# A decoder layer on one core: twelve Strassen-Winograd pairs in its MLP in place of ten, with the order of the first pieces and of the last products changed

## What is computed

```python
ff = jnp.square(jax.nn.relu(x @ w_ff1)) @ w_ff2      # w_ff1 1024 x 4096, w_ff2 4096 x 1024
x = layer_norm(2 ** 0.25 * x + ff, ln3_g, ln3_b)
```

## Time and profile before

| | before |
|---|---|
| median of 3 runs | 400.83 us (400.57 to 403.71) |
| profiled execution, device time | 401.14 us |
| its span, first to last instruction | 399.3 us |
| mean granted TensorE clock | 0.996 |
| TensorE busy | 390.9 us, 98% |
| VectorE busy | 330.2 us, 83% |
| ScalarE busy | 251.3 us, 63% |
| HBM read | 76.97 MB |

### The profile page before, as it was taken

One profiled execution on the slowest core, in us unless ns is written; L12 is line 12 of the kernel. 1 busy time (PEld: TensorE's weight loads), 2 busy tenths in 40 slices (PEclk: granted clock), 3 DMA queues, 4 the chain that ended last, 5 costly groups with the idle time before them and its releaser, 6 DMA issues.

```text
span 399.3 us, 5666 instructions
## 1 busy us (share of the span) xinstructions
PE 390.9 (98%) x2118; PEld 334.8 (84%) x2118; DVE 330.2 (83%) x430; ACT 251.3 (63%) x335; POOL 74.1 (19%) x71
## 2 busy tenths in 40 slices
PE   8999999999999999999999999999999999999993
PEld 6888888889888888899988888888888888888872
DVE  5599595999988896878567776999798979999896
ACT  6666569666464628555733776787687767776720
POOL 2059400047860105000005101000000000000000
PEclk9999999999999999999999999999999999999998
DMA  8997737734646390755353266775776575667002
GB/s 286 376 379 264 252 116 249 259 128 139 243 146 213 106 313 5 243 179 191 126 200 126 97 236 213 238 235 214 236 231 190 202 253 175 219 220 251 2 0 105
DMA packets 24449, 78.39 MB, mean 196 GB/s; under 512 B 1670, under 2 KB 3046, under 8 KB 20326
## 3 DMA queue, kind: packets, MB, share of 16 engines
q1 hardware_dynamic: 22592, 75.24, 52.5%
q0 software_dynamic: 1440, 2.62, 4.5%
q10 hardware_dynamic: 390, 0.17, 0.2%
HBM read 76.97 MB, written 1.05 MB: 195 GB/s over the span
## 4 chain that ended last, share of the span: by engine, by line
PE 81%; DMA 8%; DVE 6%; ACT 2%; issue 2%; DVEq 0%; ACTq 0%
PE bank L1560 15%; PE bank L1561 15%; PE bank L1562 15%; PE bank L1634 12%; PE bank L1963 7%; DMA raw<-in_w_ff 7%; PE bank L1638 6%; PE bank L1970 4%; DVE w_lo L1400 2%; PE bank L1786 2%; DVE w_lo L1394 1%; PE bank L1566 1%; DMA raw<-in_lead 1%; PE bank L1740 1%; DVE actB L1462 0%
## 5 line engine op out<-in xcount | busy, mean ns | idle before, releaser
L1011 DVE TENSOR_TENSOR w_lo<-raw,w_hi 128x2048 fp32r<-128x2048 f32 x30 | 70.6, 2360 | 10.9 <-ACT w_hi L609 10.8
L609 ACT CAST w_hi<-raw 128x2048 fp32r<-128x2048 f32 x32 | 60.7, 1913 | 15.9 <-PE bank L1562 14.3
L1963 PE MATMUL bank<-actA,w_hi 128*128 128x512 f32 x224 | 55.6, 391 | 0.0
L1963 PEld LDWEIGHTS bank<-actA,w_hi 128*128 128x128 f32 x224 | 41.9, 188 | 8.9 <-ACT const L918 0.3
L1560 PE MATMUL bank<-w_hi,actB 128*128 128x512 f32 x109 | 43.4, 398 | 0.0
L1561 PE MATMUL bank<-w_lo,actB 128*128 128x512 f32 x109 | 42.7, 391 | 0.0
L1562 PE MATMUL bank<-w_hi,actB 128*128 128x512 f32 x109 | 42.6, 391 | 0.0
L1560 PE MATMUL bank<-w_hi,actA 128*128 128x512 f32 x96 | 38.0, 396 | 0.0
L1562 PE MATMUL bank<-w_hi,actA 128*128 128x512 f32 x96 | 37.5, 391 | 0.0
L1561 PE MATMUL bank<-w_lo,actA 128*128 128x512 f32 x96 | 37.5, 390 | 0.0
L1634 PE MATMUL bank<-actA,w_hi 128*128 128x512 f32 x140 | 34.4, 392 | 0.0
(11 more groups left out here) (241 smaller groups left out, 864.2 us busy)
## 6 DMA issues: line engine op xcount, KB each, us to landing
raw<-in_w_ff SPq DMA_DIRECT2D x32, 1024.0 KB, 6.0
raw<-in_w_in SPq DMA_DIRECT2D x10, 1024.0 KB, 6.9
raw<-in_w_xkv SPq DMA_DIRECT2D x8, 1024.0 KB, 5.0
raw<-in_w_mix_o SPq DMA_DIRECT2D x4, 1024.0 KB, 4.9
raw<-in_w_xq SPq DMA_DIRECT2D x4, 1024.0 KB, 5.0
raw<-in_w_xo SPq DMA_DIRECT2D x4, 1024.0 KB, 5.0
raw<-in_w_ff POOLq DMA_DIRECT2D x10, 256.0 KB, 6.3
raw<-in_lead SPq DMA_DIRECT2D x6, 384.0 KB, 5.4
```

Source lines behind the costliest of these rows:

```text
L609: act.copy(dst, half_view(u)).then_inc(hi_done, 1)
L1011: dve.tensor_tensor(dst, half_view(u), hi_part.bitcast(f32), ALU.subtract).then_inc(lo_done, 1)
L1963: pe.matmul(b[:, :].rearrange("p (h s) -> p h s", h=2), hi[:, k, m * P:(m + 1) * P], actA[:, :, k, :], start=k == 0, stop=False, skip_grou ...
```

## The change

`KINDS` becomes `CCSSSSSCSSSSSSSL`: S pairs 2 to 6 and 8 to 14, C pairs 0, 1 and 7, one L pair (15). So `LAST_S` is 14, and the loops of ScalarE and VectorE have 13 passes. T3 DMAs on GpSimd become twelve. TensorE's pass 14 has no up blocks. In VectorE's passes `up_low(q+3)` stands ahead of `weight_sums(q+1)`. `hidden_low(15)` stands ahead of all combining of products, and `LAST_ORDER` has P5 ahead of P3. Among the first pieces `hidden_low(0)` goes ahead of `hidden_sums(1)`, and on ScalarE `hidden_high(0)` ahead of `empty(2, 0)`, `empty(2, 1)` ahead of `down_high(1)`.

```diff
--- before.py
+++ after.py
@@ -39,7 +39,7 @@
 WARM_UP = [512, 512, 128]
 PAIRS = 16
 A21, A11, A22, A12 = range(4)
-KINDS = "CCSSSCSSSCSSSSLL"
+KINDS = "CCSSSSSCSSSSSSSL"
 S_PAIRS = [q for q in range(PAIRS) if KINDS[q] == "S"]
 S_A = {"A11": 0, "A22": 1, "A12": 2, "S3": 3, "S1": 4, "S2": 5, "S4": 6}
 C_A = {"A21": 0, "A11": 1, "A22": 2, "A12": 3, "D1": 4, "D2": 5}
@@ -54,7 +54,7 @@
 P_BANK = {"P1": 0, "P2": 3, "P3": 2, "P4": 1, "P5": 4, "P6": 5, "P7": 6}
 UP_BANK = [7, 6, 0, 5]
 ORDER = ["P1", "P2", "P7", "P3", "P5", "P6", "P4"]
-LAST_ORDER = ["P1", "P2", "P6", "P3", "P5", "P7", "P4"]
+LAST_ORDER = ["P1", "P2", "P6", "P5", "P3", "P7", "P4"]
 LAST_S = S_PAIRS[-1]
 
 
@@ -970,11 +970,11 @@
             seed_product("P2", 1, 1, ALPHA)
             first_hidden(0)
             first_hidden(1)
+            hidden_high(0)
             empty(2, 0)
-            hidden_high(0)
             hidden_high(1)
+            empty(2, 1)
             down_high(1)
-            empty(2, 1)
             for q in range(1, LAST_S):
                 up_high(q + 3)
                 square(q + 1)
@@ -983,17 +983,11 @@
                 hidden_high(q + 1)
                 wsum_high(q + 1)
                 empty(q + 2, 1)
-            up_high(LAST_S + 3)
-            square(LAST_S + 1)
-            empty(LAST_S + 2, 0)
-            hidden_high(LAST_S + 1)
-            down_high(LAST_S + 1)
+            square(PAIRS - 1)
+            hidden_high(PAIRS - 1)
             act.wait_ge(wsum_lo, len(S_PAIRS))
             act.wait_ge(product_done, 1)
             act.copy(first_product, bank[P_BANK["P1"]][:, :]).then_inc(p1_copied, 1)
-            empty(LAST_S + 2, 1)
-            square(LAST_S + 2)
-            hidden_high(LAST_S + 2)
 
 
         @block.vector
@@ -1482,22 +1476,20 @@
             first_square(1)
             up_low(3)
             hidden_sums(0)
+            hidden_low(0)
             hidden_sums(1)
-            hidden_low(0)
             hidden_low(1)
             down_low(1)
             add_halves(2)
             for q in range(1, LAST_S):
+                up_low(q + 3)
                 weight_sums(q + 1)
-                up_low(q + 3)
                 hidden_sums(q + 1)
                 down_low(q + 1)
                 hidden_low(q + 1)
                 wsum_low(q + 1)
                 add_halves(q + 2)
-            up_low(LAST_S + 3)
-            hidden_low(LAST_S + 1)
-            down_low(LAST_S + 1)
+            hidden_low(PAIRS - 1)
 
             def product(name):
                 dve.wait_ge(product_done, LAST_ORDER.index(name) + 1)
@@ -1507,11 +1499,9 @@
             dve.wait_ge(p1_copied, 1)
             dve.tensor_tensor(b, b, first_product, ALU.add).then_inc(corner_done, 1)
             link(dve.tensor_tensor(sixth_less_first, product("P6"), first_product, ALU.subtract))
-            add_halves(LAST_S + 2)
             link(dve.tensor_tensor(with_fifth, product("P5"), sixth_less_first, ALU.add))
             b = product("P3")
             dve.tensor_tensor(b, b, with_fifth, ALU.add).then_inc(corner_done, 1)
-            hidden_low(LAST_S + 2)
             link(dve.tensor_tensor(with_seventh, product("P7"), sixth_less_first, ALU.add))
             link(dve.scalar_tensor_tensor(left_rest, X[:, 0, 0:512], ALPHA, with_seventh, ALU.mult, ALU.add))
             dve.tensor_tensor(bank[P_BANK["P7"]][:, :], product("P5"), left_rest, ALU.add).then_inc(corner_done, 1)
@@ -2020,42 +2010,35 @@
             multiply_plain(0, 1)
             for q in range(1, LAST_S + 1):
                 order = ORDER if q < LAST_S else LAST_ORDER
-                up_block(q + 2, 0)
+                if q < LAST_S:
+                    up_block(q + 2, 0)
                 if KINDS[q] == "S":
                     multiply(q, order[:4])
                 else:
                     multiply_plain(q, 0)
-                up_block(q + 2, 1)
+                if q < LAST_S:
+                    up_block(q + 2, 1)
                 if KINDS[q] == "S":
                     multiply(q, order[4:])
                 else:
                     multiply_plain(q, 1)
 
-            def corner(n, q):
+            def corner(n):
 
                 name, t, c = [("P2", 1, 1), ("P3", 1, 0), ("P7", 0, 0), ("P4", 0, 1)][n]
                 pe.wait_ge(corner_done, n + 1)
-                pe.wait_ge(a_lo, q + 1)
-                if q == PAIRS - 1:
-                    pe.wait_ge(up_lo, PAIRS - 1)
-                else:
-                    pe.wait_ge(down_raw_lo, q + 1)
-                a = blocks[q % 3]
+                pe.wait_ge(a_lo, PAIRS)
+                pe.wait_ge(up_lo, PAIRS - 1)
+                a = blocks[(PAIRS - 1) % 3]
                 for m in range(2):
                     block_at = (2 * m + t) * P
-                    if q == PAIRS - 1:
-                        mov = [v[:, 1, 0, m * 1024 + c * 512:m * 1024 + (c + 1) * 512] for v in (w_hi, w_lo)]
-                    else:
-                        b = 512 * RAW_B[f"B{m + 1}{2 - c}"]
-                        mov = [v[q % 2][:, b:b + 512] for v in (down_hi, down_lo)]
+                    mov = [v[:, 1, 0, m * 1024 + c * 512:m * 1024 + (c + 1) * 512] for v in (w_hi, w_lo)]
                     i = three(bank[P_BANK[name]][:, :], [a[:, at0 + block_at:at0 + block_at + P] for at0 in (0, 896)],
-                              mov, False, q == PAIRS - 1 and m == 1, on=True)
-                if q == PAIRS - 1:
-                    i.then_inc(corner_full, 1)
-
-            for n, q in [(0, PAIRS - 2), (1, PAIRS - 2), (0, PAIRS - 1), (1, PAIRS - 1),
-                         (2, PAIRS - 2), (2, PAIRS - 1), (3, PAIRS - 2), (3, PAIRS - 1)]:
-                corner(n, q)
+                              mov, False, m == 1, on=True)
+                i.then_inc(corner_full, 1)
+
+            for n in range(4):
+                corner(n)
 
 
 def kernel(**inputs):
```

## The result

The changed kernel takes 403.48 us (median of 16 runs), the kernel before 400.76 (16 runs beside it). The ratio is 1.0058, 95% interval 1.0042 to 1.0073: 0.6% slower, clear of noise though small. That is 2.3 us, as far as the two mean times lie apart; the medians lie 2.7 us apart, since the kernel before scatters upward, to 403.71. One of the 16 executions of the changed kernel took 435.75 us at a mean granted clock of 0.849, where the others had 0.992 or more, and is left out of the ratio and the mean. The forecast was 402.9 us, +2.1 us.

The account below looks back on a forecast made before the run. TensorE bounds the loop, VectorE close behind; -2.0 us from TensorE, overrun by VectorE's 4.1, gives +2.1: 403.2 us for the profiled execution, 402.9 in the median's terms. Forecast's own range 401.9 to 404.0, whole range 399.8 to 405.0.

Parts of the forecast that it names:

- TensorE, -1.4 us in the loop and no stall: TensorE's loop: two plain pairs become seven-product pairs, saving 1.4 us; pair 14 starts at 380.5, no stall before 385.
- just in time: Pair 14's third product on TensorE: wants the low part of its weight sums at 381.9, which is there at 381.8.
- A VectorE pass of 10.59 against 10.35: MLP loop: an S pair costs VectorE 10.59 us and TensorE 10.35 us.
- The restart 8.1 us behind a pair's first product: VectorE's loop: a pass never starts before 8.1 us after the previous pair's first product, since up_low needs ScalarE's up_high.
- s(13): Start of VectorE's pass 13, forecast at 371.7 us.
- VectorE is not late: Rival at pairs 8 and 9: up_high does not hold VectorE up; -0.3 us, 400.5 us; chance 0.17.
- T3 DMAs no longer waited for: VectorE's weight_sums: load and T3 get 16.1 us, 13.9 before; waits of 6.5 us in total become 0.
- the rival in which they come late: weight_sums from pair 9 on: load and T3 at 17.0 us lose 0.9 each two passes; +4.8, 405.6 us; chance 0.13.
- The end: VectorE's tail: combining 3.31 us after add_halves(15) starts, last statistics 10.2 us later at 395.2, +2.1 us.
- First pieces and `LAST_ORDER` at 0: Start of the loop and last products: reordering the first pieces, and P5 ahead of P3, gain 0.
- TensorE only: Rival at the end: the count of matmuls decides, combining begins by 383.4; -2.0 us, 398.8 us; chance 0.08.
- The clock: Rival in the tail: TensorE's gaps bring 1.2 GHz, corner matmuls take 0.46 us each; +4.1, 404.9 us; chance 0.04.

Follow-up runs that it names:

- e2: The changed kernel with only KINDS edited, so the plain pair between stands at pair 11 and not 7, still twelve S pairs: 402.32 us.
- e4: The changed kernel with only KINDS edited, plain pairs at 5 and 9, so eleven S pairs: 403.48 us.
- e3: The changed kernel with weight_sums(q+1) ahead of up_low(q+3) again in VectorE's passes, as in the kernel before: 406.90 us.
- e8: The changed kernel with the order of the first pieces of the kernel before: 403.14 us.
- e6: The changed kernel with P3 ahead of P5 again in LAST_ORDER, as in the kernel before: 403.47 us.
- e5: The changed kernel with the edits of e1 and e2 together: 401.15 us.
- e1: The changed kernel with hidden_low(15) behind the add that finishes corner P3, and ScalarE's copy of P1 ahead of square(15) and hidden_high(15): 401.40 us.
- e9: e7 with the two output stores of token half 1 issued by ScalarE and not SyncE: 400.30 us.
- e7: e5 with hidden_low(15) ahead of the add finishing corner P3, and token half 1's last layer-norm step moved from VectorE to ScalarE and GpSimd: 400.31 us.

## Why the prediction was right, point by point

- **TensorE, -1.4 us in the loop and no stall.** Right: pair 14 starts 122.08 us behind pair 2 (forecast 122.1), and TensorE's rows list no wait between pair 0 and the corners. The one thing to see is the third product of pair 14, which starts 0.30 us behind the matmul ahead of it (382.22, 382.52) where 0.23 is usual: it is the place that the forecast called just in time.
- **A VectorE pass of 10.59 against 10.35.** Right: 372.30 - 361.71 = 10.59.
- **The restart 8.1 us behind a pair's first product.** Right, and the step on which all hung. s(13) was forecast at 371.7; 372.30 less the 0.56 of the mark is 371.74. Pass 7 starts at 308.54, 8.14 behind pair 6's first product at 300.40, and its wait for L884 is in the row. At pair 9 the two bounds were 0.2 apart, and the pass ahead of it indeed takes 10.78 (319.14 to 329.92) and not 10.59. But only 0.04 of it lies where the forecast looked, in front of `up_low`; most, 0.13, lies in front of `down_low`, which waits for ScalarE's `down_high` (322.45 + 1.91). Timelines of VectorE and ScalarE:

```profile
324.06 0.29 DVE L1450 TENSOR_TENSOR qk<-qk 128x128 f32<-128x128 f32 x1
324.40 2.29 DVE L1394 TENSOR_TENSOR w_lo<-raw,w_hi 128x2048 fp32r<-128x2048 f32 x1
```
```profile
322.45 1.91 ACT L898 CAST w_hi<-raw 128x2048 fp32r<-128x2048 f32 x1
```

  In other passes the first two start 0.21 apart, here 0.34. e2 and e4 moved the place and count of the plain pairs and gave what the rule says. The rival "VectorE is not late" needed this wait to be absent.
- **T3 DMAs no longer waited for.** Right, and priced by e3 at 3 us or more. Load and T3 DMA landed after at most 8.2 and 7.3 us in the changed kernel, as before; the rival in which they come late found no case.
- **The end.** Right: combining 3.31 us behind the last `add_halves` (385.61 - 382.30), last statistics 10.16 later (forecast 10.2). Sum forecast +2.1; 2.13 from the mark. TensorE's last corner was placed to end near 393 (last matmul from 393.08).
- **First pieces and `LAST_ORDER` at 0.** Right (e8, e6). TensorE's wait ahead of pair 0 is 0.21 after and 0.20 before.
- **The rival "TensorE only"** was costed wrongly: for last statistics at 391.1, combining has to begin 10.2 us earlier, at 380.9 and not by 383.4. Its adds need products of pair 14, which itself only starts at 380.5; in e5 the first add waits for one. So its time was out of reach for any order of VectorE's work that keeps those 10.2 us.
- **The clock.** TensorE waited 0.39 us at two corners, where matmuls start 0.78 us apart and not 0.23, and the granted clock stayed at full, 2.4 GHz. Windows of the changed kernel, columns as in the earlier trace rows, with the DMA engines' share and GB/s behind the clock:

```profile
386.00:388.00 2.00, 1.85 (x7) 1.05 (x6) 1.93 (x4) 0.00 (x0) 0.00 (x0) 1.00 0.00 0
388.00:390.00 2.00, 1.61 (x7) 1.05 (x6) 1.93 (x4) 0.00 (x0) 0.00 (x0) 1.00 0.00 0
390.00:392.00 2.00, 1.61 (x8) 1.29 (x8) 2.00 (x4) 0.00 (x0) 0.00 (x0) 1.00 0.00 0
392.00:393.00 1.00, 1.00 (x6) 0.84 (x5) 0.93 (x4) 0.00 (x0) 0.30 (x1) 1.00 0.00 0
```

  It fell only once TensorE had nothing left to do (mean 0.86 in the window from 395 to 396, 0.50 behind it). By the rule of the Trainium skill (TensorE: Matmul & The Clock Gate, section HAM oscillation) idle gaps of TensorE can bring the slower clock back; the trace doesn't show it for gaps this short.
- **Off by 0.6 in the absolute time** (402.9 against 403.48, and 403.2 against 403.80 for the profiled executions): in the profiled execution the MLP starts later by the 0.56 of the mark, which is nearly all of it. Whether the other executions have it too no trace shows. It arises between 15 and 34 us, in code common to both, and I didn't find its cause; the traces of e1 to e9 have it between -0.27 and +0.71, so I count it neither to the change nor against it.

## What to carry to other kernels

When two engines run a loop at nearly the same pace (here 10.35 against 10.59 us), write down the recurrence of the slower one with the wait that caps its lead: work saved ahead of the last such wait was worth nothing here (e4, e8), and only the passes behind it counted (e2). The last iteration has no successor to hide under, so a chain across engines (here add, square, high part, low part, 3.3 us) belongs behind work that is already there and not in front of it. And an order of instructions inside a pass can be worth more than the work that one set out to save: 2.2 us of room for a DMA were worth 3 us (e3), while the six matmuls, 1.4 us by their count, showed in no time until the end had been rebuilt as well: e1, with all of them saved, can't be told from the kernel before.

## What the runs showed of the hardware that was not expected

- The 256 KB output stores: with three of them in flight together (e7) the time from the last statistics to the end rose from 6.2 to 6.8 us, at 342 GB/s over the three, and issuing two from another engine (e9) changed nothing (400.30 against 400.31 us).
- ScalarE's multiply by a per-partition inverse root took 0.6 us a half and GpSimd's add of 128 x 512 1.26 us at the end of e7, while VectorE ran its own instructions at the distances of the changed kernel (1.32 us from statistics to aggregate and from one pair of layer-norm steps to the next): neither cost VectorE anything there that the timeline shows. ScalarE read PSUM and GpSimd read SBUF twice; VectorE's larger instructions at that time read one PSUM bank and at most one wide SBUF operand.
